# Gram products of an RWKV-7 scan, cut into row halves of 64 over 64x64 tiles of the array

## The chip, the cores and the metric

One core of a Trainium2 chip runs the whole program. The metric is the device time of one execution in microseconds (us). A time quoted for a kernel is the median of several executions, and one execution was taken with the hardware profiler.

## What is computed

The reference is one inference step of a trunk layer over 384 tokens (128 of context, 256 of latents): a conditioned norm, one large input projection, two token mixers side by side (Mamba-2 and RWKV-7), an output projection, and a mixture of experts. The part that matters here is the RWKV-7 scan, 16 heads of width 64, run forwards and backwards:

```python
def wkv7_scan(r, w, k, v, kk, a, s0):
    def step(s, inp):
        r_t, w_t, k_t, v_t, kk_t, a_t = inp
        sa = jnp.einsum('bhij,bhj->bhi', s, kk_t)
        s = s * w_t[:, :, None, :] - sa[..., None] * (kk_t * a_t)[:, :, None, :] + v_t[..., None] * k_t[:, :, None, :]
        return s, jnp.einsum('bhij,bhj->bhi', s, r_t)
    ...
```

## The kernel before

The program is straight-line code, written out by hand for each engine; the order in which it is written is the order in which an engine executes it, and semaphores join the engines. Everything is in float32. One product in the code (one row of an order listing) is four instructions in the trace: two weight loads (PEld, LDWEIGHTS) and two matmuls (PE, MATMUL), which are the two passes of a float32 product.

The scan is computed in chunks of 128 tokens: three tiles of tokens, each in two directions. It goes through **eight rounds** (called 0 to 7 here), one for each pair of heads; the heads lie in partitions 0 to 63 and 64 to 127. `round_pe` is a round's work on TensorE, `round_act` and `round_dve` are its work on ScalarE and VectorE. Inside a round there are three independent sets s = 0, 1, 2 (a direction and a tile each), and the chain goes back and forth:

- `compact_grams` (L522, L529) forms small Gram blocks in 32 and 64 row pieces of the array; ScalarE copies them, VectorE transposes them.
- Four levels l = 1 to 4 of a triangular inverse follow: 48 products of 32x32 (`blocks_32`, L568), a copy by ScalarE, 48 more, a masked copy and a transpose by VectorE.
- Then the halves are joined (L581 to L680) and the right-hand sides, updates, states and outputs follow (L693 to L747).

Between these steps TensorE is given work that does not depend on them: `mamba_out` (L616, one 128x512 product of the Mamba output, rounds 1 to 6), `fill(...)`, which prepares the next pair of heads or finishes the last one (L477, L482, L487 to L505; round 0 has none of the last pair, round 7 none of the next), and **`gram_pair(p)`** for p = 0 to 4, the full Gram products that are needed later. `gram_pair(0)` stands behind `compact_grams`, 1 and 2 and 3 behind levels 1, 2 and 3, and 4 inside level 4. It writes to `gram_bank(p, h)`, one bank of PSUM for each head h. Behind each, VectorE's `gram_unit(p)` (L971, L974, L980) multiplies the two banks with a triangular mask `tri` of zeros and ones and writes the result to `gk` or `gb`.

`gram_pair` with p < 3 makes, for each direction d and head h, one product of `kap` (64 rows, 128 columns of weights) with both halves of `arr` (256 columns); with p = 3 and 4 it makes for three sets, directions and heads one product of `be` with one half of `arr` (128 columns). A head's 64 rows are one half of the array's rows, so that the two heads' products run in two row tiles of 64x128. `p < 3` holds 4 products each, p = 3 holds 8, and p = 4 holds 4.

Of the kernel before, what the change touches and what calls it, by code (L numbers as in the profile page):

```python
# [17 lines left out]
P = 128  # L18
# [84 lines left out]
def program(nc, a, out):  # L103
    ctx = ExitStack()
    with ctx:
# [6 lines left out]
        ps = ctx.enter_context(nc.psum_tensor("ps", [P, 8, 512], F32))  # L112
# [70 lines left out]
        def at(flat, o, *shape):  # L183
            names = "abcd"[:len(shape)]
            n = 1
            for x in shape:
                n *= x
            v = flat[:, o:o + n]
            return v if len(shape) == 1 else v.rearrange(
                f"p ({' '.join(names)}) -> p {' '.join(names)}", **dict(zip(names, shape)))  # L190
# [24 lines left out]
        be = at(misc, 6144, 2, NTILE, P)  # L215
        kap = at(misc, 6912, 2, NTILE, P)
# [317 lines left out]
        def gram_bank(p, h):  # L534
            return 2 * ((2 * p + h) % 3)

        def gram_pair(pe, c, arr, p):

            if p == 0:
                pe.wait_ge(inv_sb, c * 9 + 2)  # L540
            else:
                if p == 1:
                    pe.wait_ge(inv_sb, c * 9 + 3)
                pe.wait_ge(gram_rd, c * 10 + (2 * p - 1))
            if p < 3:
                for d in range(2):
                    j = TJ[p][d]
                    for h in range(2):
                        k = slice(64 * h, 64 * h + 64)
                        mm = pe.matmul(ps[:, gram_bank(p, h), 256 * d:256 * d + 256], kap[k, d, j, :],  # L550
                                       arr[k, d, j, :, :].rearrange("p a t -> p (a t)"), start=True, stop=True)
            else:
                for i, s in enumerate(((0, 1), (2,))[p - 3]):
                    for d in range(2):
                        j, o = TJ[s][d], P * (2 * i + d)
                        for h in range(2):
                            k = slice(64 * h, 64 * h + 64)
                            mm = pe.matmul(ps[:, gram_bank(p, h), o:o + P], be[k, d, j, :], arr[k, d, j, 1, :],
                                           start=True, stop=True)
            mm.then_inc(gram_ps, 1)  # L560

        def blocks_32(pe, s, o, lhs, rhs):
# [56 lines left out]
        def round_pe(pe, c, b, prev, nxt):  # L619
# [11 lines left out]
            for s in range(3):  # L631
                pe.wait_ge(yo_rd, c * 3 + (s + 1))
                compact_grams(pe, arr, s)
            gram_pair(pe, c, arr, 0)
            fill(MEAN)
            for l in range(1, 5):
                for s in range(3):
                    pe.wait_ge(x_ok, c * 15 + (3 * l - 3 + s + 1))
                    blocks_32(pe, s, 0, diag(s), xc[s]).then_inc(yl_ps, 1)
                mamba_out(pe, c, 2 * l - 2)  # L640
                if l > 1:
                    fill({2: KSQ, 3: W_UP + 1, 4: A_UP + 1}[l])
                if l == 4:
                    gram_pair(pe, c, arr, 4)
                for s in range(3):
                    pe.wait_ge(yl_ok, c * 12 + (3 * l - 3 + s + 1))
                    if l > 1:
                        pe.wait_ge(xT_ok, c * 12 + (3 * l - 6 + s + 1))
                    blocks_32(pe, s, P, xcT[s], yc[s]).then_inc(zl_ps, 1)
                mamba_out(pe, c, 2 * l - 1)  # L650
                if l in (2, 3):
                    fill({2: W_UP, 3: A_UP}[l])
                if l < 4:
                    gram_pair(pe, c, arr, l)
                if l == 1:
                    fill(VAR)
# [2010 lines left out]
```

## Time and profile before

| | |
|---|---|
| median of 3 runs | 1230.35 us (1223.66 to 1233.05) |
| the profiled execution | 1230.25 us |
| its span, first to last instruction | 1228.4 us |
| TensorE matmuls (PE) | 1128.7 us busy, 92% of the span, x15671 |
| weight loads (PEld) | 727.9 us, 59%, x15671 |
| VectorE (DVE) | 560.9 us, 46% |
| ScalarE (ACT) | 338.4 us, 28% |
| mean granted TensorE clock | 0.952 of full speed |

The span is read as one line of time, from 0 to 1228.4 us. The rounds lie between about 421 and 835 us. Busy times of matmuls are modelled and overlap each other, so what a stretch of TensorE's work costs is read from the start of its first instruction to the start of the next group's first. "issue" as a releaser means that the engine waited for nothing that the profile shows.

### The profile page before, as it was taken

What the parts mean: (1) busy time and instruction counts of PE and PEld (TensorE: products, weight loads), DVE (VectorE), ACT (ScalarE), POOL (GpSimd) and SP (SyncE); (2) the same over time, 40 slices, a digit from 0 to 9 for tenths busy, and PEclk for the clock granted to TensorE, in tenths of its full rate; (3) what the DMA queues carried; (4) which work ended last, traced back from release to release, by engine and by line L of the source; (5) the groups of instructions that cost most, each with busy time, mean ns of one, the idle gap of its engine ahead of it and who ended that gap; (6) DMA issues with size and microseconds to landing.
All of it is one profiled execution on the core that took longest, in us unless ns stands there. A gap on an engine that the chain in (4) does not pass through costs nothing.

```text
span 1228.4 us, 34668 instructions
## 1 busy us (share of the span) xinstructions
PE 1128.7 (92%) x15671; PEld 727.9 (59%) x15671; DVE 560.9 (46%) x1301; ACT 338.4 (28%) x712; POOL 139.6 (11%) x186
## 2 busy tenths in 40 slices
PE   5899889999999879998999989889999999999991
PEld 3555336677766566666666666675585555555540
DVE  0355102567766655766656667531662212222215
ACT  2022101322224354534545345321330000000012
POOL 6000001023103030312303023000000000000002
PEclk9899988999999879999999989879999999999996
DMA  9533555332208301120211201203286999999874
GB/s 333 208 137 137 205 205 161 103 86 69 69 4 145 57 10 38 45 69 22 70 38 44 65 18 47 106 3 109 76 352 240 407 416 416 416 415 416 340 286 169
DMA packets 83665, 201.28 MB, mean 164 GB/s; under 512 B 12484, under 2 KB 27079, under 8 KB 78919
## 3 DMA queue, kind: packets, MB, share of 16 engines
q1 hardware_dynamic: 79392, 186.97, 42.7%
q10 hardware_dynamic: 3271, 9.08, 1.8%
q0 software_dynamic: 864, 3.15, 0.8%
q8 instruction: 116, 1.90, 0.6%
q14 instruction: 22, 0.18, 0.0%
HBM read 183.97 MB, written 15.20 MB: 162 GB/s over the span
## 4 chain that ended last, share of the span: by engine, by line
PE 87%; DVE 3%; DMA 3%; issue 3%; ACT 2%; POOL 0%; POOLq 0%; SPq 0%; DVEq 0%; ACTq 0%; PEldq 0%
PE ps L1641 16%; PE ps L1228 10%; PE ps L1217 7%; PE ps L568 5%; PE ps L1248 5%; PE ps L616 4%; PE ps L1684 4%; PE ps L1876 3%; PE ps L550 2%; PE ps L1764 2%; PE ps L1780 2%; PE ps L482 2%; DMA ring_a<-in_w_in 1%; PE ps L600 1%; PE ps L1603 1%
## 5 line engine op out<-in xcount | busy, mean ns | idle before, releaser
L1641 PE MATMUL ps<-hT,ring_a 128*128 128x384 f32 x624 | 213.2, 497 | 3.4 <-DVE hT L2249 2.5
L1641 PEld LDWEIGHTS ps<-hT,ring_a 128*128 128x128 f32 x624 | 118.3, 194 | 83.9 <-issue 7.2
L1217 PE MATMUL ps<-scratch,misc 128*128 128x128 f32 x864 | 99.7, 275 | 0.1
L1217 PEld LDWEIGHTS ps<-scratch,misc 128*128 128x128 f32 x864 | 97.9, 192 | 1.9 <-issue 1.9
L568 PEld LDWEIGHTS ps<-ring_a 32*32 32x32 f32 x6144 | 64.0, 108 | 41.0 <-issue 28.4
L2331 DVE SCALAR_TENSOR_TENSOR um_a<-ps,mum,um_a 128x252 f32<-128x252 f32 (+1 forms) x162 | 57.2, 409 | 65.5 <-ACT um_a L2035 64.5
L568 PE MATMUL ps<-ring_a 32*32 32x32 f32 x6144 | 72.5, 197 | 12.8 <-issue 12.8
L1228 PE MATMUL ps<-ring_a,um_a 128*64 128x512 f32 x288 | 63.4, 593 | 1.4 <-DVE um_a L1271 1.4
L1283 DVE COPY um_a<-ps 128x256 f32<-128x256 f32 x17 | 7.2, 425 | 125.5 <-PE ps L1237 125.5
L1508 POOL TENSOR_TENSOR mixm<-tri,la 128x512 f32<-128x512 f32 x24 | 28.4, 1209 | 271.7 <-DVE la L2301 187.2
L1228 PE MATMUL ps<-misc,um_a 128*64 128x512 f32 x128 | 56.3, 592 | 1.4 <-DVE um_a L1271 1.4
L1295 ACT ACTIVATE um_a<-ps 128x1024 f32<-128x1024 f32 x17 | 17.4, 1026 | 143.0 <-PE ps L1248 143.0
L616 PE MATMUL ps<-ring_a,mixm 128*128 128x512 f32 x96 | 54.0, 644 | 0.0
L1684 PE MATMUL ps<-ring_a,hT 128*128 128x512 f32 x96 | 46.8, 648 | 6.9 <-DMA ring_a<-in_w_in 6.9
L1271 DVE COPY um_a<-ps 128x1024 f32<-128x1024 f32 x17 | 20.8, 1224 | 70.4 <-PE ps L1217 69.6
L2035 ACT ACTIVATE um_a<-ps,mum 128x384 f32<-128x384 f32 x27 | 15.7, 582 | 128.2 <-PE ps L1641 128.2
L1582 POOL DMA_INDIRECT um_a<-expert_rows,wdt x6 | 6.7, 1123 | 360.7 <-DMA expert_rows<-um_a 354.9
L1228 PEld LDWEIGHTS ps<-ring_a,um_a 128*64 128x64 f32 x288 | 21.0, 137 | 41.9 <-issue 41.9
L999 DVE COPY_PREDICATED ring_a<-lvl,ps 128x128 f32<-128x128 int32 x96 | 26.6, 277 | 39.3 <-PE ps L568 39.0
L1289 ACT ACTIVATE um_a<-ps 128x256 f32<-128x256 f32 x17 | 6.5, 385 | 122.5 <-PE ps L1228 122.5
L1603 PE MATMUL ps<-ring_a,cond 128*32 128x512 f32 x192 | 28.2, 712 | 12.6 <-DMA ring_a<-in_w_ada 10.1
L1684 PEld LDWEIGHTS ps<-ring_a,hT 128*128 128x128 f32 x96 | 19.6, 208 | 31.0 <-issue 23.9
(420 smaller groups left out, 2020.4 us busy)
## 6 DMA issues: line engine op xcount, KB each, us to landing
ring_a<-in_w_ada SPq DMA_DIRECT2D x12, 2048.0 KB, 12.5
ring_a<-in_w_in SPq DMA_DIRECT2D x11, 2048.0 KB, 9.0
ring_a<-in_moe_w_gate SPq DMA_DIRECT2D x18, 1024.0 KB, 9.9
ring_a<-in_moe_w_up SPq DMA_DIRECT2D x18, 1024.0 KB, 11.9
ring_a<-in_moe_w_down SPq DMA_DIRECT2D x18, 1024.0 KB, 12.0
ring_a<-in_w_out SPq DMA_DIRECT2D x48, 256.0 KB, 2.8
expert_rows<-um_a ACTq DMA_DIRECT2D x17, 512.0 KB, 7.1
misc<-in_moe_w_gate SPq DMA_DIRECT2D x16, 512.0 KB, 9.4
```

Of the source, the lines that this page charges most:

```text
L568: mm = pe.matmul(ps[r, 2 * s + 1, m:m + 32], lhs[r, h, d, :], rhs[r, h, d, :], start=True, stop=True, tile_position=(32 * q, 32 * q), skip ...
L616: pe.matmul(ps[:, 7, :], mixm[:, k, P * (r // 2):P * (r // 2) + P], mamba_w[n % RING], start=(k == 0), stop=(k == KT - 1)).then_inc(half_p ...
L999: dve.copy_predicated(xc[s], level_mask(l, False), ps[:, 2 * s + 1, P:2 * P].rearrange("p (h d q) -> p h d q", h=2, d=2)).then_inc(x_ok, 1)
L1217: mm = pe.matmul(ps[:, k // 4, P * (k % 4):P * (k % 4) + P], h2[:, j, P * k:P * k + P], pick[:, j, :], start=(j == 0), stop=(j == NTILE - 1))
L1228: mm = pe.matmul(ps[h, 2 + b, :], xgT[:, b, k, h], gate_up_tile(b, x, k), start=(k == 0), stop=(k == KT - 1), tile_position=(0, CH * x), s ...
L1248: mm = pe.matmul(ps[h, 5 + c, :], hidT[:, b, k, h], wdn[b][x][:, k, BLK * c:BLK * c + BLK], start=(k == 0), stop=(k == 1), tile_position=( ...
L1508: ins = pool.tensor_tensor(lam[:, j, 4 * d:4 * d + 4, :], tri[:, 2 - 2 * d, :].unsqueeze(1).to_broadcast([P, 4, P]), la[:, j, h:h + 4].uns ...
L1603: mm = pe.matmul(ps[32 * q:32 * q + 32, ada_bank(i), :], cond[:, 2 * q + k2, :], slot(n)[:, 2 * q + k2, :], start=(k2 == 0), stop=(k2 == 1 ...
L1641: mm = pe.matmul(ps[:, t % 4 if isinstance(t, int) else t, 0:T], slot(n)[:, k, P * c:P * c + P], hT[:, k, :], start=(k == 0), stop=(k == K ...
L1684: mm = pe.matmul(ps[:, i % 4, :], hT[:, k, P * j:P * j + P], slot(n)[:, k, :], start=(k == 0), stop=(k == KT - 1))
L1876: mm = pe.matmul(ps[:, 2 * j + c, :], um_a[:, k, P * j:P * j + P], wout_tile(k)[:, BLK * c:BLK * c + BLK], start=(k == 0), stop=(k == KT - 1))
L2331: ins = dve.scalar_tensor_tensor(dst, src, mum[:, m, t:t + 1], dst, ALU.mult, ALU.add)
```

## The change

In `gram_pair` each product is split into two by rows of the result, z = 0 and 1, of 64 rows each. The weights of a product are then 64x64, and it is put at a tile position (64h, 64z): four tiles of 64x64 instead of two of 64x128. A row half that sees only a part of the columns through the triangular mask is multiplied with this part alone: `seen_from` gives all 128 columns where z = d, and 64 of them where z differs. What lies outside is not written; `gram_unit` still reads it and multiplies it with zero. The other engines' code is the same, and so are all waits and increments.

```diff
@@ -534,6 +534,13 @@
         def gram_bank(p, h):
             return 2 * ((2 * p + h) % 3)
 
+        def half_rows(z):
+            return slice(64 * z, 64 * z + 64)
+
+        def seen_from(z, d):
+
+            return slice(0, P) if z == d else slice(64 - 64 * d, P - 64 * d)
+
         def gram_pair(pe, c, arr, p):
 
             if p == 0:
@@ -545,18 +552,23 @@
             if p < 3:
                 for d in range(2):
                     j = TJ[p][d]
-                    for h in range(2):
-                        k = slice(64 * h, 64 * h + 64)
-                        mm = pe.matmul(ps[:, gram_bank(p, h), 256 * d:256 * d + 256], kap[k, d, j, :],
-                                       arr[k, d, j, :, :].rearrange("p a t -> p (a t)"), start=True, stop=True)
+                    for z in range(2):
+                        r, t = half_rows(z), seen_from(z, d)
+                        for h in range(2):
+                            k = slice(64 * h, 64 * h + 64)
+                            mm = pe.matmul(ps[r, gram_bank(p, h), 256 * d:256 * d + 256].rearrange("p (a t) -> p a t", a=2)[:, :, t],
+                                           kap[k, d, j, r], arr[k, d, j, :, t], start=True, stop=True,
+                                           tile_position=(64 * h, 64 * z), skip_group_check=True)
             else:
                 for i, s in enumerate(((0, 1), (2,))[p - 3]):
                     for d in range(2):
                         j, o = TJ[s][d], P * (2 * i + d)
-                        for h in range(2):
-                            k = slice(64 * h, 64 * h + 64)
-                            mm = pe.matmul(ps[:, gram_bank(p, h), o:o + P], be[k, d, j, :], arr[k, d, j, 1, :],
-                                           start=True, stop=True)
+                        for z in range(2):
+                            r, t = half_rows(z), seen_from(z, d)
+                            for h in range(2):
+                                k = slice(64 * h, 64 * h + 64)
+                                mm = pe.matmul(ps[r, gram_bank(p, h), o + t.start:o + t.stop], be[k, d, j, r], arr[k, d, j, 1, t],
+                                               start=True, stop=True, tile_position=(64 * h, 64 * z), skip_group_check=True)
             mm.then_inc(gram_ps, 1)
 
         def blocks_32(pe, s, o, lhs, rhs):
```

The first place is the start of a round on TensorE, round 1 here: the last pieces of `compact_grams` (L529), `gram_pair(0)`, the mean of the last pair (L505) and level 1 (L568, L616). Before:

```order
L529 MATMUL ps<-scratch,misc 64x64 x4
L550 MATMUL ps<-scratch,misc 128x256 x4
L505 MATMUL ps<-hT,bones 128x384
L568 MATMUL ps<-ring_a 32x32 x48
L616 MATMUL ps<-ring_a,mixm 128x512
L568 MATMUL ps<-ring_a 32x32 x48
L616 MATMUL ps<-ring_a,mixm 128x512
L550 MATMUL ps<-scratch,misc 128x256 x4
```

The same place on TensorE after the change (the lines behind `gram_pair` have numbers 12 higher, so L568 is L580 and L616 is L628):

```order
L529 MATMUL ps<-scratch,misc 64x64 x4
L559 MATMUL ps<-scratch,misc 64x256 x2
L559 MATMUL ps<-scratch,misc 64x2x64 x4
L559 MATMUL ps<-scratch,misc 64x256 x2
L505 MATMUL ps<-hT,bones 128x384
L580 MATMUL ps<-ring_a 32x32 x48
L628 MATMUL ps<-ring_a,mixm 128x512
L580 MATMUL ps<-ring_a 32x32 x48
L628 MATMUL ps<-ring_a,mixm 128x512
L559 MATMUL ps<-scratch,misc 64x256 x2
L559 MATMUL ps<-scratch,misc 64x2x64 x4
L559 MATMUL ps<-scratch,misc 64x256 x2
```

Four products of 256 columns became eight: four of 256 columns and four of 64 columns twice (2x64). Nothing else moved.

The second place is level 3 and 4 of the same round, where a product of the next pair's low-rank decay (L482) stands just ahead of `gram_pair(3)` and `gram_pair(4)`. Before:

```order
L482 MATMUL ps<-um_a,stw 128x384
L558 MATMUL ps<-scratch,misc 128x128 x8
L568 MATMUL ps<-ring_a 32x32 x48
L616 MATMUL ps<-ring_a,mixm 128x512
L482 MATMUL ps<-um_a,stw 128x384
L558 MATMUL ps<-scratch,misc 128x128 x4
L568 MATMUL ps<-ring_a 32x32 x48
L616 MATMUL ps<-ring_a,mixm 128x512
```

The same place on TensorE after the change, up to the second half of level 4:

```order
L482 MATMUL ps<-um_a,stw 128x384
L570 MATMUL ps<-scratch,misc 64x128 x2
L570 MATMUL ps<-scratch,misc 64x64 x4
L570 MATMUL ps<-scratch,misc 64x128 x4
L570 MATMUL ps<-scratch,misc 64x64 x4
L570 MATMUL ps<-scratch,misc 64x128 x2
L580 MATMUL ps<-ring_a 32x32 x48
L628 MATMUL ps<-ring_a,mixm 128x512
L482 MATMUL ps<-um_a,stw 128x384
L570 MATMUL ps<-scratch,misc 64x128 x2
L570 MATMUL ps<-scratch,misc 64x64 x4
L570 MATMUL ps<-scratch,misc 64x128 x2
```

Eight products became sixteen and four became eight, behind the same L482. A round has 24 products of `gram_pair` before and 48 after.

## Rows read from the trace of the kernel before

**Rows 1.** Page: span; part 3 (packets, MB, share of 16 engines); part 4.

```profile
span 1228.4 us, 34668 instructions
...
q8 instruction: 116, 1.90, 0.6%
...
PE 87%; DVE 3%; DMA 3%; issue 3%; ACT 2%; POOL 0%; POOLq 0%; SPq 0%; DVEq 0%; ACTq 0%; PEldq 0%
```

**Rows 2.** Windows, rounds 1, 2 and 6: length, busy us (xinstructions) by engine, clock.

```profile
475.61:524.07 48.46, 47.15 (x1471) 32.49 (x1470) 33.15 (x79) 24.00 (x58) 10.29 (x10) 1.00 0.17 51
524.07:575.48 51.41, 48.74 (x1471) 33.71 (x1470) 32.71 (x79) 24.21 (x58) 10.28 (x10) 0.97 0.18 49
...
731.93:780.60 48.67, 47.34 (x1471) 32.49 (x1469) 32.97 (x79) 24.00 (x58) 9.77 (x9) 1.00 0.23 80
```

**Rows 3.** Waits of PE (total, times, longest): round 0; rounds 2-5 (three rows); round 7.

```profile
PE ps L568 <- issue: 4.3, 5, 1.3
...
PE ps L600 <- issue: 3.1, 3, 1.6
PE ps L568 <- issue: 2.8, 4, 1.5
PE ps L594 <- issue: 2.0, 2, 1.2
...
PE ps L568 <- issue: 5.7, 5, 2.4
```

**Rows 4.** Windows between two issue waits: first of eight, and their sum.

```profile
427.87:431.43 3.56, 2.44 (x128) 1.91 (x128) 3.03 (x10) 0.28 (x1) 0.00 (x0) 1.00 0.02 5
...
sum 30.76, PE 19.93 PEld 16.17 DVE 18.13 ACT 8.37 POOL 1.47; mean PE 2.49 PEld 2.02 DVE 2.27 ACT 1.05 POOL 0.18
```

**Rows 5.** Windows: round 1 from its first Gram product to the joined halves.

```profile
474.65:508.52 33.87, 33.72 (x1155) 21.64 (x1145) 24.78 (x57) 16.01 (x40) 8.45 (x6) 1.00 0.22 67
```

**Rows 6.** Timeline of PE in round 1: start, us to the end, group.

```profile
475.27 0.35 PE L529 MATMUL ps<-scratch,misc 64*64 64x64 f32 x8
475.61 1.14 PE L550 MATMUL ps<-scratch,misc 64*128 64x256 f32 x8
476.67 0.91 PE L505 MATMUL ps<-hT,bones 128*128 128x384 f32 x2
477.51 1.04 PE L568 MATMUL ps<-ring_a 32*32 32x32 f32 x96
478.49 1.12 PE L616 MATMUL ps<-ring_a,mixm 128*128 128x512 f32 x2
479.54 1.04 PE L568 MATMUL ps<-ring_a 32*32 32x32 f32 x96
...
488.26 0.59 PE L482 MATMUL ps<-um_a,stw 64*128 64x384 f32 x1
488.27 0.70 PE L550 MATMUL ps<-scratch,misc 64*128 64x256 f32 x2
...
489.96 1.05 PE L568 MATMUL ps<-ring_a 32*32 32x32 f32 x96
...
495.00 0.59 PE L482 MATMUL ps<-um_a,stw 64*128 64x384 f32 x1
...
496.74 1.04 PE L568 MATMUL ps<-ring_a 32*32 32x32 f32 x96
...
498.77 0.59 PE L482 MATMUL ps<-um_a,stw 64*128 64x384 f32 x1
...
500.05 1.06 PE L568 MATMUL ps<-ring_a 32*32 32x32 f32 x96
```

**Rows 7.** Timeline of DVE in round 1, behind level 2.

```profile
486.84 0.30 DVE L999 COPY_PREDICATED ring_a<-lvl,ps 128x128 f32<-128x128 int32 x1 [2.77 <-PE ps L568]
```

**Rows 8.** Windows as in Rows 2: round 2 ahead of and in a clock drop.

```profile
554.02:557.43 3.41, 2.18 (x82) 1.69 (x82) 3.31 (x5) 1.82 (x7) 3.31 (x2) 1.00 0.02 5
557.43:560.84 3.41, 3.41 (x50) 2.69 (x48) 0.70 (x3) 2.70 (x9) 1.71 (x5) 0.50 0.21 58
```

## The prediction

> **What bounds the kernel now.** I read the page's chain first: TensorE carries 87% of it [rows 1]. So what counts is what becomes of TensorE's own time in the eight rounds, the only place that the change touches. The windows by round come second. A round holds the same work from 1 to 6, 1471 matmuls and as many loads, yet round 1 took 48.46 us, round 6 48.67 and round 2 51.41 [rows 2]. The reader should ask where the 3 us come from, since nothing in the program differs.
>
> The waits answer it. In rounds 2 to 5 TensorE stood still for "issue", that is for no semaphore, nine times in all, 7.9 us together; in round 0 4.3 us in five waits at L568 alone, in round 7 5.7 us in five [rows 3]. In rounds 1 and 6 that view lists none. The waits fall in the middle of a group of equal products, so it isn't data that is late. Their distance tells what is: between two neighbouring waits lie 128 matmuls and 128 weight loads [rows 4], 256 instructions, and the instruction queue brought 1.90 MB in 116 packets, 16.4 KB each [rows 1]. TensorE waits for its own program. A block of 256 instructions is brought by one packet, and the next block is there only some time after the last was entered. Eight windows from one such wait to the next sum to 30.76 us [rows 4], 3.85 us a block; the first of them took 3.56.
>
> This price stands against the work that a block holds. In round 1, 2300 instructions, nine blocks, ran from the first Gram product to the joined halves in 33.87 us, with TensorE busy for 33.72 [rows 5]: 3.76 us a block, already as much as a fetch costs. The levels are the dense part: 96 matmuls and as many loads, three quarters of a block, start within 0.98 us (477.51 to 478.49 [rows 6]). So TensorE has two bounds here that lie within a few per cent: the time of its products and the number of its instructions.
>
> **The change part by part.** *Products.* The price of a group is read from its start to the next one's. L505, two passes of 384 columns, took 0.84 us (476.67 to 477.51), L616, two passes of 512, 1.05 (478.49 to 479.54) [rows 6]. That is 0.21 for 256 more columns, 0.82 ns a column, and a fixed 0.21. It gives 1.05 for L550, whose row tiles each take four passes of 256; 1.06 was measured (475.61 to 476.67). L529 shows that four 64x64 tiles run at once: two passes of 64 columns on each, in 0.34 at most (475.27 to 475.61), where the formula gives 0.32 for four tiles at once and 0.42 if two shared a row half in turn.
>
> After the change a tile takes, for p < 3, two passes of 256 and two of 128 columns: 768, 0.63 + 0.21 = 0.84 us. The sixteen products of p = 3 give the same 768 and 0.84; p = 4 has half, 0.52. With p = 0 and 1 the group stands alone: 1.06 becomes 0.84, twice -0.22. With p = 2, 3 and 4 it stands behind L482 and now runs beside it, in the other row half (L550 starts at 488.27, 10 ns behind L482 [rows 6]); both together take 1.70 (488.26 to 489.96), 1.74 (495.00 to 496.74) and 1.28 (498.77 to 500.05). I take it that the other tile shape ends this overlap. L482 has L505's columns, so 0.84: 1.68, 1.68 and 1.36, that is -0.02, -0.06 and +0.08. Sum -0.44 a round; with the overlap kept it would be some tenths more, so I take -0.5, or -4 us in eight rounds.
>
> The Trainium skill (TensorEngine Tiling, Key Properties) says that a change of the tiling mode drains TensorE; by it the overlap goes, as I assumed, and the fixed 0.21 between groups of different shapes agrees. No run here shows 64x128 products beside 64x64 ones.
>
> *Other engines.* VectorE gets its Gram banks earlier and does the same work; behind level 2 it waited 2.77 us for TensorE [rows 7]. So a TensorE that gains is not stopped by it, and one that loses delays everything.
>
> *Instructions.* 24 products of a round become 48. One product is four instructions, so a round gains 96: 0.375 of a block, at 3.85 us a block **1.44 us**, if the fetch is what TensorE waits for. All of them lie in the dense part, and the shorter products raise the rate further: round 1 would hold 9.375 blocks in 33.4 us, 3.56 a block. That is as short as the first of the eight windows and 8% under their mean [rows 4].
>
> Bounds of this cost: nothing, if fetches keep up (-4 us for the whole change), and 8 x 1.44 = +11.5, if every round is bound by the fetch and the saved product time is lost in waits.
>
> *The sum.* Rounds 0 and 7 are bound already, with little fill between the levels: 2 x 1.44 = +2.9. Rounds 2 to 5 wait about 2 us each: +1.44 each, less 0.2 where a block isn't bound and keeps its gain, +5.0. Rounds 1 and 6 lie between -0.5, if fetches keep up, and 9.375 x 3.76 - 33.87 = +1.4, if they cost what they can at most have cost there before. I take +1.0, nearer to the second, because only one block is fetched ahead: a dense block waits though the mean would allow it. +2.0. Together +9.9 us. Against the profiled execution's own 1230.25 us that is **1240 us**, and this execution stands at the median (1230.35) of the three shown.
>
> **The rivals.**
>
> *The fetch keeps up, the product time is saved.* For it: rounds 1 and 6 had no issue waits [rows 2], and the 0.375 blocks more could find room in the tail of a round, where larger products stand. Against it: the added instructions aren't in the tail, and the waits are in the part where they are [rows 3]. 1230.25 - 4 = **1226 us**. It decides from a fetch of under 3.56 us a block in the dense part. The Trainium skill (Runtime: NRT & Kernel Launch, Instruction fetch mechanics) gives blocks of 256 instructions, the next one fetched while the current one runs, at a cost that is "mostly hidden". This rival is its case. The block size agrees with the trace; that it is hidden does not, with 7.9 us of waits in rounds 2 to 5.
>
> *The waits bring the clock down too.* In round 2 a stretch of 3.41 us in which TensorE was busy for 2.18 was followed by 3.41 us at a granted clock of 0.50, 1.2 GHz [rows 8]; round 1 stood at 1.00 throughout [rows 2]. Such a stretch costs up to half its length, 1.7 us, where TensorE is the bound. If more waits give rounds 1 and 6 such a drop and rounds 2 to 4 a second one, that is 5 x 1.7 = 8.5 on top: **1248 us**. For it: the undisturbed rounds are those without waits. Against it: some waits had no drop behind them in the first round (the first window of [rows 4] has a clock of 1.00), and at half the clock a fetch has more time.
>
> *The column tiles don't run at once*, so the change does not do what it says: a row half then takes 1536 columns, 1.47 us for p < 3 and p = 3, 0.84 for p = 4. The five places cost +0.41, +0.41, +0.61, +0.57 and +0.40, 2.4 us a round, 19 in all: **1249 us**. L529's 0.34 speaks against it, though 64 columns are few.
>
> **How the numbers follow.** A chance of 0.52 for the forecast (1233 to 1244), 0.20 for a fetch that keeps up (1222 to 1233), 0.22 for the clock (1244 to 1255), 0.06 for the tiles. The range of 1226 to 1250 leaves out the lower half of the second case and the tops of the last two. One per cent, 12.3 us, is about what a measurement of this kernel can tell from no change. Faster than 1218 is left only to an end of the second case, 0.03; slower than 1242.7 are the clock, most of the tiles' case and the top of the forecast, 0.33; within it 0.64.
>
> **What would show it.** In the profile after: `gram_pair(0)` at about 0.84 us from start to next start; 1519 matmuls in a round; issue waits in rounds 1 and 6, of about 1 to 2 us each round, and more of them in rounds 0 and 2 to 5; 119 instruction packets, three more (8 x 96 = 768 instructions); waits still 256 instructions apart; rounds 1 and 6 no shorter than before. I am wrong if rounds 1 and 6 get half a microsecond shorter with no issue waits, if the groups take over 1.06 us, or if the time comes back outside the rounds.

## The result and the profile after

The changed kernel takes **1248.51 us** (median, 1247.02 to 1249.72) against 1227.82 us (1223.66 to 1233.05) for the kernel before, measured beside it: ratio 1.0159, interval 1.013 to 1.0188. It is slower, by 21 us. The forecast of 1240 us had the sign, its range held the time, and the time stands where the rival of the clock put it, at 1248. How it came there is another matter: two of the forecast's terms were far off, and its price for an added instruction is not a fixed one.

The page of the kernel after, in the parts that answer to [rows 1] (span; busy time of PE; the instruction queue; the chain; two groups of part 5, whose last column is idle time and what ended it):

```profile
span 1246.4 us, 35436 instructions
PE 1134.9 (91%) x16055; PEld 730.9 (59%) x16055; DVE 555.8 (45%) x1301; ACT 338.4 (27%) x712; POOL 140.3 (11%) x186
...
q8 instruction: 119, 1.95, 0.6%
...
PE 87%; issue 4%; DVE 3%; DMA 3%; ACT 2%; POOL 0%; POOLq 0%; SPq 0%; DVEq 0%; ACTq 0%; PEldq 0%
...
L580 PE MATMUL ps<-ring_a 32*32 32x32 f32 x6144 | 74.5, 198 | 24.6 <-issue 24.6
L580 PEld LDWEIGHTS ps<-ring_a 32*32 32x32 f32 x6144 | 65.1, 109 | 52.5 <-issue 40.8
```

There are 384 more matmuls and as many loads (768 instructions in eight rounds), three more instruction packets, and TensorE stood idle for 24.6 us ahead of the matmuls at L580, the 32x32 products of the levels, with no releaser that the profile shows; ahead of the same products it was 12.8 us before. L559 and L570 are the products of `gram_pair`.

Rounds 1 to 6 of the kernel after, by windows as in [rows 2] (length, busy us by engine, granted clock, DMA share, GB/s; each from the first product of `gram_pair(0)`):

```profile
468.23:522.86 54.63, 49.91 (x1520) 33.93 (x1518) 32.22 (x79) 24.21 (x58) 10.27 (x10) 0.94 0.15 46
522.86:578.25 55.39, 49.90 (x1518) 33.87 (x1518) 31.95 (x79) 24.21 (x58) 10.32 (x10) 0.94 0.15 45
578.25:632.50 54.25, 49.80 (x1519) 33.87 (x1517) 32.41 (x79) 24.17 (x58) 10.29 (x10) 0.94 0.15 46
632.50:682.61 50.11, 46.78 (x1519) 31.36 (x1517) 32.37 (x79) 23.88 (x58) 10.28 (x10) 1.00 0.16 50
682.61:739.37 56.76, 51.22 (x1520) 34.17 (x1517) 32.50 (x79) 24.19 (x58) 10.41 (x10) 0.91 0.14 44
739.37:793.72 54.35, 48.61 (x1519) 32.23 (x1517) 31.85 (x79) 23.88 (x58) 9.77 (x9) 0.97 0.21 71
```

Round 1 grew from 48.46 to 54.63 us and round 6 from 48.67 to 54.35; these had been the undisturbed ones. All six together, from the first product of `compact_grams` in round 1 to that in round 7, took 305.00 us before and 325.50 after. Two windows give the same span, the first of the kernel before, the second of the kernel after:

```profile
473.70:778.70 305.00, 290.00 (x8816) 200.18 (x8815) 198.61 (x469) 144.73 (x348) 61.69 (x60) 0.97 0.17 51
```

```profile
466.32:791.82 325.50, 296.23 (x9104) 199.44 (x9103) 193.30 (x469) 144.54 (x348) 61.84 (x60) 0.95 0.15 48
```

Those 20.5 us are the loss. The other parts of the program cancel: rounds 0 and 7 together 107.6 us against 108.4, the stretch ahead of the rounds 413.8 against 421.0, the stretch behind them 399.5 against 394.0. Ahead of the rounds the code is the same; among the kernels of this study that share it, that stretch took 412.6 to 421.7 us, so a difference of 7 us there is what one execution shows against another.

Waits of PE by releaser in the same window of the kernel after (total, times, longest):

```profile
PE ps L580 <- issue: 12.4, 11, 1.6
PE ps L593 <- issue: 5.1, 4, 1.8
PE ps L612 <- issue: 2.6, 3, 1.1
PE ps L606 <- issue: 1.6, 3, 0.7
PE ps L597 <- issue: 1.4, 2, 0.7
```

The sum is 23.1 us in 23 waits; this view of the kernel before gives 8.2 us in ten. The timeline of PE in rounds 1 to 6 of the kernel after (start, us to the end, group, idle time ahead of it) shows both what the products cost and where the waits are:

```profile
468.23 0.88 PE L559 MATMUL ps<-scratch,misc 64*64 64x256 f32 x16
469.04 0.91 PE L505 MATMUL ps<-hT,bones 128*128 128x384 f32 x2
...
473.55 0.64 PE L580 MATMUL ps<-ring_a 32*32 32x32 f32 x52 [0.96 <-issue]
...
482.90 0.91 PE L482 MATMUL ps<-um_a,stw 64*128 64x384 f32 x2
483.74 0.88 PE L559 MATMUL ps<-scratch,misc 64*64 64x256 f32 x16
484.55 1.11 PE L580 MATMUL ps<-ring_a 32*32 32x32 f32 x96
...
489.53 0.91 PE L482 MATMUL ps<-um_a,stw 64*128 64x384 f32 x2
490.37 0.90 PE L570 MATMUL ps<-scratch,misc 64*64 64x128 f32 x32
491.20 1.04 PE L580 MATMUL ps<-ring_a 32*32 32x32 f32 x96
...
493.23 0.91 PE L482 MATMUL ps<-um_a,stw 64*128 64x384 f32 x2
494.07 0.56 PE L570 MATMUL ps<-scratch,misc 64*64 64x128 f32 x16
494.57 1.06 PE L580 MATMUL ps<-ring_a 32*32 32x32 f32 x96
...
528.68 0.59 PE L580 MATMUL ps<-ring_a 32*32 32x32 f32 x45 [1.34 <-issue]
583.71 0.54 PE L580 MATMUL ps<-ring_a 32*32 32x32 f32 x39 [1.08 <-issue]
637.74 0.45 PE L580 MATMUL ps<-ring_a 32*32 32x32 f32 x32 [0.80 <-issue]
687.96 0.41 PE L580 MATMUL ps<-ring_a 32*32 32x32 f32 x26 [0.83 <-issue]
745.23 0.37 PE L580 MATMUL ps<-ring_a 32*32 32x32 f32 x19 [1.29 <-issue]
```

The six rows that end in a wait for issue are the key to the case. They are one and the same wait, in the second half of level 1 of rounds 1, 2, 3, 4, 5 and 6. The group has 96 matmuls; 52 of them stand behind the wait in round 1, then 45, 39, 32, 26 and 19. So the end of a block moves by 6.6 matmuls a round, and with their loads by 13 instructions. A round after the change has 3059 instructions in the trace (in the six rounds 9103 matmuls and as many loads, and some 25 a round without work of their own), and 3059 is 12 x 256 - 13. **A round is almost a whole number of blocks long**, and so every round meets the block ends at nearly the same places. Before, it had 96 fewer, 2963, which is 12 x 256 - 109: there the places move by 109 from round to round.

And the clock: behind a group of such waits it can fall. Windows of the kernel after, ahead of and in the drop of round 1:

```profile
499.04:502.45 3.41, 2.66 (x123) 2.18 (x124) 3.31 (x5) 2.30 (x7) 3.23 (x3) 1.00 0.02 5
502.45:509.28 6.83, 6.83 (x114) 5.41 (x110) 3.02 (x8) 4.32 (x12) 2.36 (x5) 0.50 0.12 34
```

TensorE was busy for 2.66 of 3.41 us, with a wait of 0.75 us among them, and then worked 6.83 us at 0.50, the level of 1.2 GHz, without a gap.

### The profile page after: what moved, and what is told of

It is laid out like the page before. It is cut to its first block, busy times and chain, and to the rows that moved or that the text cites. A ratio compares the mean times of both kernels' runs of the same rounds, so it can differ in the third digit from the quotient of the medians.

```text
span 1246.4 us, 35436 instructions
## 1 busy us (share of the span) xinstructions
PE 1134.9 (91%) x16055; PEld 730.9 (59%) x16055; DVE 555.8 (45%) x1301; ACT 338.4 (27%) x712; POOL 140.3 (11%) x186
## 4 chain that ended last, share of the span: by engine, by line
PE 87%; issue 4%; DVE 3%; DMA 3%; ACT 2%; POOL 0%; POOLq 0%; SPq 0%; DVEq 0%; ACTq 0%; PEldq 0%
PE ps L1653 16%; PE ps L1240 9%; PE ps L1229 7%; PE ps L580 6%; PE ps L1260 5%; PE ps L628 4%; PE ps L1696 4%; PE ps L1888 3%; PE ps L482 2%; PE ps L559 2%; PE ps L1776 2%; PE ps L1792 2%; PE ps L612 2%; PE ps L453 1%; DMA ring_a<-in_w_in 1%
## 5 line engine op out<-in xcount | busy, mean ns | idle before, releaser
L1229 PE MATMUL ps<-scratch,misc 128*128 128x128 f32 x864 | 99.6, 275 | 0.0
L1229 PEld LDWEIGHTS ps<-scratch,misc 128*128 128x128 f32 x864 | 97.9, 192 | 1.6 <-issue 1.6
L580 PE MATMUL ps<-ring_a 32*32 32x32 f32 x6144 | 74.5, 198 | 24.6 <-issue 24.6
L580 PEld LDWEIGHTS ps<-ring_a 32*32 32x32 f32 x6144 | 65.1, 109 | 52.5 <-issue 40.8
L628 PE MATMUL ps<-ring_a,mixm 128*128 128x512 f32 x96 | 55.4, 659 | 0.0
L1283 DVE COPY um_a<-ps 128x1024 f32<-128x1024 f32 x17 | 20.8, 1225 | 72.8 <-PE ps L1229 72.0
L2047 ACT ACTIVATE um_a<-ps,mum 128x384 f32<-128x384 f32 x27 | 15.7, 582 | 128.0 <-PE ps L1653 128.0
L828 ACT ACTIVATE ring_a<-ps 128x128 f32<-128x128 f32 x96 | 26.4, 277 | 43.7 <-PE ps L580 42.0
L1615 PE MATMUL ps<-ring_a,cond 128*32 128x512 f32 x192 | 25.8, 658 | 12.7 <-DMA ring_a<-in_w_ada 10.2
```

The lines of the kernel that those rows point to most:

```text
L580: mm = pe.matmul(ps[r, 2 * s + 1, m:m + 32], lhs[r, h, d, :], rhs[r, h, d, :], start=True, stop=True, tile_position=(32 * q, 32 * q), skip ...
L628: pe.matmul(ps[:, 7, :], mixm[:, k, P * (r // 2):P * (r // 2) + P], mamba_w[n % RING], start=(k == 0), stop=(k == KT - 1)).then_inc(half_p ...
L828: act.activation(yc[s].rearrange("p h d c -> p (h d c)"), ps[:, 2 * s + 1, 0:P], ACT.Copy).then_inc(yl_ok, 1)
L1229: mm = pe.matmul(ps[:, k // 4, P * (k % 4):P * (k % 4) + P], h2[:, j, P * k:P * k + P], pick[:, j, :], start=(j == 0), stop=(j == NTILE - 1))
```

## The experiments

Three theories were weighed. **A**, the forecast's own: the number of instructions sets the price, 3.85 us for each 256 where the fetch is the bound (in a narrower form, only where they stand in the dense part of a round). **B**: the row halves or the 64x64 tiles themselves cost something. **C**, formed when the first four runs were in: the number doesn't matter much, but the places at which the blocks end, and a round of 3059 instructions brings a bad place back each round. The table has what came out; rounds and waits are of one profiled execution each, over all eight rounds.

| kernel | instructions a round | block ends move by | rounds, us | issue waits, us | median, us | ratio to before (interval) |
|---|---|---|---|---|---|---|
| before | 2963 | 109 | 413.4 | 23.3 | 1227.8 | |
| after | 3059 | 13 | 433.1 | 38.8 | 1248.5 | 1.0159 (1.013 to 1.0188) |
| e1_split_columns | 3011 | 61 | 409.7 | 20.7 | 1226.2 | 0.9994 (0.9957 to 1.0031) |
| e2_split_in_the_tail | 3059 | 13 | 414.4 | 22.9 | 1233.8 | 1.004 (1.0012 to 1.0068) |
| e3_change_fewer_blocks | 2963 | 109 | 410.4 | 24.4 | 1252.4 | see the text |
| e4_before_fewer_blocks | 2867 | 205 | 400.5 | 17.0 | 1241.6 | see the text |
| e5_shift_104 | 3059 | 13 | 406.7 | 20.2 | 1236.8 | 1.0076 (1.0045 to 1.0108) |
| e6_shift_208 | 3059 | 13 | 427.0 | 35.3 | 1256.8 | 1.0206 (1.0162 to 1.0251) |
| e7_only_first_three | 3011 | 61 | 410.0 | 25.0 | 1228.5 | 0.9969 (0.9937 to 1.0001) |
| e8_identities_kept | 2915 | 157 | 399.2 | 17.7 | 1218.9 | 0.9914 (0.9885 to 0.9944) |
| e9_change_and_identities | 3011 | 61 | 410.2 | 26.8 | 1229.1 | 1.0011 (0.998 to 1.0043) |
| e10_same_count_old_tiles | 3059 | 13 | 437.6 | 26.3 | 1255.5 | 1.022 (1.0173 to 1.0267) |
| e11_same_count_shift_104 | 3059 | 13 | 417.9 | 15.7 | 1238.5 | 1.01 (1.0036 to 1.0164) |
| e12_identities_shift_104 | 2915 | 157 | 397.2 | 18.6 | 1219.1 | 0.9926 (0.9901 to 0.9952) |

### More instructions in the dense part, old tiles

The kernel before, with the products of the first three pairs cut by columns:

```diff
-    mm = pe.matmul(ps[:, gram_bank(p, h), 256 * d:256 * d + 256], kap[k, d, j, :],
-                   arr[k, d, j, :, :].rearrange("p a t -> p (a t)"), start=True, stop=True)
+    for i in range(2):
+        o = 256 * d + P * i
+        mm = pe.matmul(ps[:, gram_bank(p, h), o:o + P], kap[k, d, j, :], arr[k, d, j, i, :],
+                       start=True, stop=True)
```

> The kernel before, with each product of p < 3 cut into two by columns (128 instead of 256) in the old 64x128 tiles: 12 products, so 48 instructions, more in a round, the same columns, tile shape and product time. Theory A (the number of instructions in the dense part, through waits for the next block and the clock drops behind them) expects about half of the change's loss, 8 to 14 us over before, 1236 to 1242 us, issue waits in every round, and gram_pair(0) still at 1.06 us. Theory B (the 64x64 tiles themselves, by their drains or by the clock) expects no more than 3 us from before.

It took 1226.21 us, the same as before. A's 8 to 14 us were a miss, and with them A as it stood: here 48 instructions a round in the dense part cost nothing, with the issue waits at 20.7 us against 23.3.

### As many instructions as the change, behind the dense part

The products at L737 and L741, in the outputs at the end of a round, each cut into two of 64 columns (24 products, 96 instructions a round):

```diff
-    pe.matmul(place(h, d), vtk[:, j, hp], gk[s][:, h, d, 1, :], ...)
+    for i in range(2):
+        t = slice(64 * i, 64 * i + 64)
+        pe.matmul(place(h, d)[:, t], vtk[:, j, hp], gk[s][:, h, d, 1, t], ...)
```

> The kernel before, with 24 products of 128 columns at the end of each round (the outputs, L737 and L741) cut into two of 64 columns: 96 instructions more in a round, as many as the change adds, but in the part of the round where a block lasts 4.9 to 8.8 us and no wait for instructions stands. Theory A in its narrow form (an instruction costs only where a block is shorter than its fetch) expects 0 to 5 us over before. A wide form (every block costs its 3.85 us wherever it stands) expects 10 us or more. Theory B expects about nothing.

1233.82 us, a little slower than before (0.4%), where the change with the same number lost 1.6%. This is what A in its narrow form expected, and C has room for it too: a round has the same 3059 instructions, but up to its outputs a block end stands up to 96 instructions elsewhere than in the change. Alone it tells nothing apart.

### Fewer instructions

One in sixteen of the 32x32 products of the levels left out, in the changed kernel and in the kernel before:

```diff
-                    for q in range(4):
+                    for q in range(4 - h * d):
```

> The changed kernel with 15 of the 16 products of 32x32 in every call of blocks_32 (one of head 1, direction 1 is left out, so a part of the inverse isn't computed): 24 products fewer in a round, so that a round has as many instructions as before the change, with the 64x64 Gram products kept. Theory A expects the loss to be gone: 1221 to 1229 us, at or a little under the kernel before, since the Gram products keep their 0.5 us a round. Theory B expects it to stay, 1240 to 1250.

> The kernel before with the same 15 of 16 products of 32x32 (the same part of the inverse isn't computed): 96 instructions fewer in a round, the group's longest tile as long as it was. Theory A says that the kernel before already paid for its instructions: 8 to 15 us faster, 1213 to 1222 us, with the issue waits of rounds 2 to 5 mostly gone. If its waits were chance, or set by the transfers alone, it stays within 3 us.

Both came out slower, 1252.43 and 1241.58 us, but not in the rounds. The windows of e3's rounds and of what follows them:

```profile
417.77:828.17 410.40, 375.51 (x11711) 260.27 (x11712) 247.58 (x605) 184.45 (x449) 71.73 (x70) 0.92 0.15 46
828.17:1249.40 421.23, 379.53 (x2202) 224.47 (x2202) 119.11 (x301) 57.89 (x84) 7.28 (x10) 0.96 0.78 310
```

The stretch behind the rounds grew to 421.23 us, from 394.0 before and 399.5 after, and holds 2202 matmuls in place of 2104: other values reach the expert router, and the experts get more work (`L1229` runs 912 times, not 864). The medians say nothing on the rounds, then. Those took 410.4 us in e3 against 433.1 after, and 400.5 in e4 against 413.4 before. So e4's rounds are 12.9 us shorter, which is within the 8 to 15 that A expected of it, and e3, with 2963 instructions a round, has rounds no longer than the kernel before. A and C both have room for that; these two runs can't tell them apart.

Set against each other, they tell more. They differ by the change alone, their stretches behind the rounds are alike (421.2 and 421.1 us), and in both the block ends move on from round to round. There the change costs 10.9 us by the medians, 9.9 in the rounds.

### The same kernel with its blocks shifted

The changed kernel with 26, or 52, more of the 32x32 warm-up products that stand long ahead of the rounds, 104 or 208 instructions that compute nothing needed and move every later block end towards the start of its round:

```diff
-            tiled(32, 32, 32, 32)
+            tiled(58, 32, 32, 32)
```

> The changed kernel with 26 more tiny products (32x32) in the warm-up near the start, 104 instructions: the rounds are untouched, only the place in them at which each block of 256 ends moves by 104 instructions. Theory C: a changed round has 3059 instructions, 13 short of twelve blocks, so that a block ends at nearly the same place in every round, and the change met a bad place; a model of the fetches on the trace's own times gives about half the waits at a shift of 64 to 144. C expects the waits of rounds 1 to 6 to fall from 23 to 10-14 us, the clock drops behind them to become fewer, and the whole 1226 to 1238 us. Theory A (the number of instructions alone) and theory B (the form of the products) expect no change, 1246 to 1250.

> As e5_shift_104, with 52 tiny products, 208 instructions. Theory C: this shift is at another bad place; waits of rounds 1 to 6 as in the change or a few us more, 1244 to 1254 us. Theories A and B: 1246 to 1250. The run guards against the extra warm-up products helping by themselves.

In the rounds nothing differs from the changed kernel, not an instruction. Yet e5 took 1236.77 us, 12 less than the change, and e6 1256.78, 8 more. The 8 us of e6 don't lie in its rounds. These took 427.0 us against 433.1, with 35.3 us of waits against 38.8, so e6 stands at a bad place again; but they began at 427.9 us instead of 413.8 (in e5 at 422.0). The added products are not free: behind the warm-up TensorE's next group, L1615, begins at 34.57 us in the change, at 39.96 in e5 and at 43.52 in e6, so some 5 and 9 us of these two times are the shift's own. Rounds 1 to 6 of e5, as one window, and PE's issue waits in it:

```profile
475.48:773.18 297.70, 285.25 (x9103) 192.53 (x9102) 197.20 (x469) 143.81 (x348) 61.64 (x60) 0.99 0.17 53
```

```profile
PE ps L580 <- issue: 2.5, 8, 0.4
PE ps L612 <- issue: 1.2, 3, 0.6
PE ps L606 <- issue: 0.9, 1, 0.9
PE ps L593 <- issue: 0.5, 1, 0.5
```

5.1 us of waits against 23.1, a clock of 0.99 against 0.95, and 297.70 us against 325.50: in this execution the rounds are quicker than before the change. It was the quickest of e5's twelve (1227.28; the others went up to 1248.8, the two slowest at the lowest granted clocks, 0.934 and 0.937, and what else differed no trace shows), so by the medians only 12 of the 21 us come back. A and B give the same time for the change and e5. That the place alone is worth some 12 us is shown; it is not shown that the place is all of the loss.

### Half of the change

Only the pairs with p < 3 by row halves, the others as before (3011 instructions a round):

> The change for p = 0, 1, 2 alone: 48 instructions more in a round than before, as in e1_split_columns, now in 64x64 tiles and with the shorter product time (0.5 us a round). Theory C: a round has 3011 instructions, 61 short of twelve blocks, so the place moves on and good and bad rounds alternate as before the change: 1220 to 1230 us, by the product time 1 to 4 us under e1_split_columns. Theory A: half the loss, 1236 to 1242. Theory B (64x64 tiles): more than half, 1236 or more.

1228.51 us, no slower than before, with the 64x64 tiles in the first three groups. B falls for these groups, and so does A's half of the loss.

### The same count in the old tiles

Here all gram products of the kernel before are cut by columns, none by rows: those of e1, and for p = 3 and 4 the following. That is the change's 3059 instructions, in the same pairs, in tiles of 64x128.

```diff
-    mm = pe.matmul(ps[:, gram_bank(p, h), o:o + P], be[k, d, j, :], arr[k, d, j, 1, :],
-                   start=True, stop=True)
+    for z in range(2):
+        t = slice(64 * z, 64 * z + 64)
+        mm = pe.matmul(ps[:, gram_bank(p, h), o + 64 * z:o + 64 * z + 64], be[k, d, j, :],
+                       arr[k, d, j, 1, t], start=True, stop=True)
```

> The kernel before with all its gram products split by columns (256 to two of 128 for the first three pairs, 128 to two of 64 for the others), in its old tiles of 64 rows by 128 columns of the array: 24 products and 96 instructions more a round, in the same pairs as the change, 3059 in all, and no product by row halves. Theory C (3059 = 12 x 256 - 13, so the block ends come back to the same places, and these are bad ones): slower, like the change or a little more, since its products get no shorter: 1242 to 1256, waits for instructions in rounds 1 to 6 of 18 to 25 us (8.5 before). Theory B (the tiles of 64x64 or the row halves cost it, through their drains or what they do to TensorE's clock): 1224 to 1234.

> e10 with 26 more of the small warm-up products at the start (104 instructions), as in e5_shift_104: 3059 instructions a round and the old tiles, but every block end 104 instructions earlier in the round. Theory C: the loss of e10 goes for the greater part, 1228 to 1240. Theory A: as e10 (the count is the same).

1255.53 us, and 1238.54 with 104 instructions more ahead: a fall of 17 us, where the change to e5 was 12. Rounds 1 to 6, first in e10, then in e11:

```profile
475.09:801.91 326.82, 304.61 (x9103) 218.71 (x9102) 193.03 (x469) 144.28 (x348) 61.59 (x60) 0.96 0.16 48
```

```profile
476.73:783.88 307.15, 295.91 (x9103) 212.47 (x9102) 196.95 (x469) 143.56 (x348) 61.67 (x60) 0.99 0.16 51
```

The issue waits of PE in these windows fall from 16.0 to 3.8 us. So a price for the place, 20 us in these two traces, is paid in the old tiles too, and it isn't the tiles'. From the change to e5 the windows differ by 28, but e5's trace was its quickest execution, while e11's (1238.62) stands at the median. One expectation was wrong: the products don't stay as long as they were. In e10's round 1 `gram_pair(3)` with L482 ahead of it:

```profile
497.26 0.91 PE L482 MATMUL ps<-um_a,stw 64*128 64x384 f32 x2
498.01 2.00 PE L562 MATMUL ps<-scratch,misc 64*128 64x64 f32 x32
499.95 1.04 PE L572 MATMUL ps<-ring_a 32*32 32x32 f32 x96
```

2.69 us, where [rows 6] have 1.74 and the change 1.67 with as many products. With the other groups (1.19, 1.19, 1.84 and 1.67 us) that is 1.74 us a round more than before, which over eight rounds would be 14 of the 27 us by which e10 is slower than the kernel before. Its waits for instructions, 16.0 us in rounds 1 to 6, stayed a little under the 18 that I had expected, which longer products may explain. Only the pair e10 and e11, with equal products, tells of the place alone.

### Without the identity products

The half-joining step (L585) adds identities by 12 products a round, 48 instructions. Here the identities are kept in `merge`, and VectorE's copy leaves them alone (a predicated copy of 294 ns for one of 283):

```diff
-            for q in range(4):
-                r = slice(32 * q, 32 * q + 32)
-                mm = pe.matmul(ps[r, 2 * s + q % 2, 0:64], i32[r, :], i32[r, :].unsqueeze(1).to_broadcast([32, 2, 32]), ...)
...
-                dve.tensor_copy(merge[...],
+                dve.copy_predicated(merge[...],
+                    other[:, :, :].bitcast(I32).unsqueeze(2).to_broadcast([P, 2, 2, 32]),
                     by_head(s, 0, 64)...).then_inc(inv_j, 1)
```

In the kernel before, in the changed one, and in the kernel before with the shift of e5:

> The kernel before, unchanged in what it computes, without the 12 products of a round that only copy an identity through PSUM (L585): the identities are written once into the tile that they go to, and VectorE's copy becomes a predicated one that leaves them. 48 instructions fewer in a dense place of each round. Theories A and C both expect fewer waits: rounds 1 to 6 shorter by 3 to 8 us in all, rounds 0 and 7 by 0.7 us each, 1218 to 1226 us. If a predicated copy takes clearly longer than the copy (0.3 us), VectorE may give some of it back.

> The changed kernel without the 12 identity products of a round (the predicated copy of e8 in their place): 3011 instructions a round instead of 3059, so the place of the block ends moves by 61 from round to round, as in e7, and no longer stands still. Theory A (the number of instructions sets the price): 48 more a round than before without a loss of time in products, 0.19 block x 3.85 us x 8 = +5.7, products -0.57 x 8 = -4.6: about before, 1226 to 1236. Theory B (the row halves themselves cost): 1240 or more. Theory C (the place of the block ends): about before on average over the places, less the products: 1212 to 1225, about like e8_identities_kept (1218.91).

> e8_identities_kept (the kernel before without the 12 identity products of a round, 2915 instructions a round) with 26 more of the small warm-up products at the start, as in e5_shift_104: every block end stands 104 instructions earlier in the round. Theory C, as far as it goes for a round whose length is far from a whole number of blocks: 2915 = 11 x 256 + 99, so the place moves by 99 from round to round and passes over all places in either kernel; a shift by 104 is about a shift by one round and moves the time little: 1214 to 1224, and the gain of e8 is of its fewer instructions and of products that are gone. Rival (e8 had by luck the better places in its eight rounds, as e9_change_and_identities had not): 1225 to 1236, like before.

On the kernel before it gives 1218.91 us and, shifted, 1219.07: **faster than both kernels**, than the one before by 0.9%, and e12 says that it isn't by luck of its place: 2915 instructions move the block ends by 157 from round to round, and the shift leaves the time as it was. On the change it gives 1229.12, no faster than before. By C I had expected 1212 to 1225, a miss; A's 1226 to 1236 held. The windows over all eight rounds show why, in e1, e7 and e9 in turn, which have 3011 instructions a round, so that their rounds begin at the same places of a block:

```profile
416.04:825.71 409.67, 378.08 (x11903) 278.27 (x11903) 250.77 (x605) 184.69 (x449) 71.88 (x70) 0.95 0.15 46
```

```profile
418.41:828.42 410.01, 374.40 (x11903) 267.31 (x11903) 249.96 (x605) 184.62 (x449) 71.93 (x70) 0.93 0.15 46
```

```profile
418.93:829.12 410.19, 371.65 (x11904) 259.79 (x11904) 248.14 (x605) 184.78 (x449) 71.86 (x70) 0.93 0.14 46
```

The busy time of TensorE falls from 378.1 to 371.7 us, and the rounds take 409.7, 410.0 and 410.2. What the products gain, the issue waits take back: 20.7, 25.0 and 26.8 us. At this number of instructions, shorter products bring nothing. In this respect A's picture of the fetch as a second bound holds, and I had let it fall too far after e1. From e8 to e9, two kernels that differ by the change alone, the medians grow by 10.2 us and the rounds by 11.0, much as from e4 to e3.

## Why the prediction was right, and where it was wrong

**The products: right.** `gram_pair(0)` went from 1.06 to 0.81 us (468.23 to 469.04), predicted 0.84; with L482 ahead the three later groups take 1.65, 1.67 and 1.34, predicted 1.68, 1.68 and 1.36. So four tiles of 64x64 run at once, and that rival is out. The overlap with L482 ended. The Trainium skill (TensorEngine Tiling (Array Packing), Key Properties) says that a change of the tiling mode drains TensorE, and the trace agrees: L559 and L570 start 0.84 us behind L482, where L550 had started 10 ns behind it [rows 6]. The sum is -0.56 us a round against the -0.5 taken.

**What the instructions are: right.** There are 1519 matmuls in a round's window, counted as in [rows 2], 119 packets, and issue waits in rounds 1 and 6. Those of round 1 are 3.7 us long together (0.96, 1.01, 1.02 and 0.75), more than the 1 to 2 expected. Two readings were a little off: rounds 2 to 5 of the kernel before had a tenth wait, of 0.3 us, beside the nine, and 3.56 us is 7%, not 8%, under the mean of the eight windows.

**The price of the instructions: wrong as a fixed price.** The step that failed is "a round gains 96: 0.375 of a block, at 3.85 us a block 1.44 us". It takes the mean of eight windows for a price that any added instruction pays. The windows go from 3.31 to 4.31 us, and not all are set by the fetch. The second and the sixth of them:

```profile
431.43:434.74 3.31, 2.28 (x127) 1.58 (x126) 1.74 (x6) 2.90 (x5) 0.00 (x0) 1.00 0.02 5
799.62:803.66 4.04, 3.81 (x128) 3.41 (x128) 2.95 (x10) 0.21 (x1) 0.00 (x0) 0.56 0.02 4
```

In the sixth, at a granted clock of 0.56, TensorE's own work fills 3.81 of the 4.04 us. Then the runs: e1 paid nothing for 48 instructions, and e5, in its quickest execution, nothing in rounds 1 to 6 for 96, where the change paid 20.5 us. Between these lie the two pairs whose block ends move on, e4 to e3 and e8 to e9, with some 10 us for the change. That is the size of the forecast's 9.9, but it is no price of each instruction, since e1 and e7 paid nothing for half as many; how much of it is due to the number of instructions and how much to the tiles no run tells.

By this picture a block costs TensorE only what its own work is shorter than the fetch, and which work falls into one block depends on where it ends. The number counts also by what it does to that place, round after round. That 3059 is 13 short of twelve blocks was there to be read from the 96, the instructions of a round and the distance of the waits, and I did not work it out.

**The sum: wrong in its parts.** Rounds 0 and 7, called bound already, were to lose 2.9 us and gained 0.8; their issue waits went only from 15.1 to 15.7 us. Rounds 1 to 6 were to lose 7.0 and lost 20.5: waits +14.9 (8.2 to 23.1), products -3.4 (six times -0.56), and the remaining 9.0 with the clock. A forecast near the time with such parts is partly luck.

**The clock: a rival that came along.** It was put at five drops more and 8.5 us, and this was about right. The mean granted clock of rounds 1 to 6 went from 0.97 to 0.95, with rounds 1 and 6, formerly at 1.00, now at 0.94 and 0.97. The trace's records of the clock add up to 34.1 us at 0.50 in the window of rounds 1 to 6, against 17.1 before. These 17 us more are what five drops like that of [rows 8] come to, and at half the clock they are worth up to 8.5 us, next to the remaining 9.0. They lie otherwise than supposed: by the clocks of the six windows most in round 5 and none in round 4. What a drop takes can be read from rounds 3 and 4 of the kernel after: 54.25 us with 0.94 and 50.11 with 1.00, 4.1 apart, of which 1.2 are the difference of their waits (3.4 against 2.2). That leaves 2.9 us for 6.8 us at half the clock. It isn't a case of its own beside the forecast, as I had it, but came along with the waits: the same shift that takes the waits away brings the clock back to 0.99 in e5 and e11.

**The fetch that keeps up: out.** The Trainium skill (Runtime: NRT & Kernel Launch, Instruction fetch mechanics) calls the cost of a block's crossing "mostly hidden". In the trace after, it isn't, with 38.8 us of issue waits in eight rounds; in rounds 1 and 6 of the kernel before it was. In e1, which paid nothing for its instructions, the waits stayed too, at 20.7 us.

**What stays open.** By the medians the shift to e5 gives back 12 of the change's 21 us, and some 5 of the other 9 may be its own warm-up products. What the rest is made of is not shown, nor is it for the 10 of the two pairs. Why these places are bad and those 104 instructions earlier good was not taken apart; that the bad ones are those where a block holds most of the 32x32 products and few of the wide ones is only an argument. Nor was it settled why e5 varies by 21 us from execution to execution, and why the stretch behind the rounds took 5.5 us more after the change. The change has no code there, and in the kernels of this study that compute the same results that stretch took 393.9 to 402.0 us.

## What to carry to other kernels

Where an engine's instructions run nearly as fast as they are brought, count a loop's or a round's instructions in the trace and take them modulo the block (256 here): near a whole number the same place comes back each time, a bad one (the change, e6, e10) or a better one (e5, e11). Some hundred idle instructions ahead of the loop tell whether it is that. Look at the loop itself, since the idle instructions cost time too, and try more than one shift and execution, since a shift can meet another bad place (e6) and executions can differ by as much (e5). Before believing that a change of products made a kernel slower or faster, run it shifted by some 100 instructions too. And where waits for instructions exist, taking products away altogether pays (0.9% for 12 of some 740 a round), while making them shorter may not.

## What the runs showed of the hardware

Small products that compute nothing needed, put near the start (25 to 43 us), far ahead of the rounds (from some 420 us on), moved the time of one and the same program from 1248.5 to 1236.8 and 1256.8 us; its rounds took 433.1, 406.7 and 427.0 us. In tiles of 64x128, sixteen products of 64 columns took 1.94 us (e10, 498.01 to 499.95), though eight of 128 columns, the same work, took with all of L482 only 1.74 [rows 6]. In 64x64 tiles sixteen products, half of them of 128 columns, took 0.83 us (490.37 to 491.20 after the change). A weight load has a median of 188 ns in e10's group; that the loads set the pace there was not tested.
